# Where the mixing norm's scale per token is multiplied in, in a fp32 kernel of a three-block network

## The reference, cut to what matters

```python
def rmsnorm(x, w):
    xf = x.astype(jnp.float32)
    y = xf * lax.rsqrt(jnp.mean(xf * xf, axis=-1, keepdims=True) + EPS)
    return (y * w.astype(jnp.float32)).astype(x.dtype)

def second_block(x, norm_mix_w, w_in, ...):
    h = x                                   # x is layer_norm(DN_ALPHA * x + y, ln_g, ln_b)
        hn = rmsnorm(h, norm_mix_w[i])      # the mixing norm
        proj = hn @ w_in[i]
        q, k, v, z, xbc, dt_raw = jnp.split(proj, SPLITS, axis=-1)
        att = chunk_band_attention(q, k, v, rel_bias[i])
        ssd = ssd_mixer(z, xbc, dt_raw, conv_w[i], conv_b[i], dt_bias[i], ...)
        h = h + jnp.concatenate([att, ssd], axis=-1) @ w_out[i]
```

## Time and profile before

| what | value |
|---|---|
| time, 3 runs | 786.69, 787.38 (median), 789.47 us |
| the profiled execution's own time | 786.68 us |
| its span in the trace | 784.9 us (1.8 us lie around it) |
| PE, DVE, ACT, POOL busy | 98%, 66%, 53%, 12% of the span |
| PE's granted clock, mean | 0.997 of full speed |
| the seam, from the last product of the second layer to the first of the convolution's | 435.50 to 452.50 us |

### The profile page before, as it was taken

The page is one execution under the profiler, slowest core; times in us unless marked ns, Lnnn a source line. Parts: engine busy times, 40 slices in busy tenths (PEclk is TensorE's granted clock), DMA queues, the critical chain, the costliest instruction groups (busy, mean ns, idle before and its releaser), DMA issues.

```text
span 784.9 us, 13096 instructions
## 1 busy us (share of the span) xinstructions
PE 770.0 (98%) x5084; PEld 676.7 (86%) x5084; DVE 514.9 (66%) x816; ACT 414.7 (53%) x623; POOL 95.6 (12%) x69
## 2 busy tenths in 40 slices
PE   8999999999999999999999899999999999999997
PEld 8998877799988887999787799899777999999996
DVE  6995656666664658478866774886756755555554
ACT  5544445454664453445765667466655544444443
POOL 2241000000100013111400208500000000000002
PEclk9999999999999999999999999999999999999999
DMA  9865643344754644776732464643216576556541
GB/s 331 316 221 174 209 161 110 118 163 114 225 205 161 208 147 134 230 229 197 250 87 82 160 210 131 198 136 134 101 60 215 189 222 208 183 193 206 174 158 53
DMA packets 77051, 137.43 MB, mean 175 GB/s; under 512 B 7104, under 2 KB 15552, under 8 KB 76992
## 3 DMA queue, kind: packets, MB, share of 16 engines
q1 hardware_dynamic: 75744, 132.15, 51.9%
q0 software_dynamic: 1248, 4.46, 1.7%
HBM read 132.80 MB, written 1.05 MB: 171 GB/s over the span
## 4 chain that ended last, share of the span: by engine, by line
PE 89%; DVE 4%; issue 2%; POOL 2%; ACT 1%; DMA 1%; SPq 0%; POOLq 0%; ACTq 0%; DVEq 0%
PE acc L1069 13%; PE acc L1071 13%; PE acc L1070 13%; PE acc L1077 12%; PE acc L1079 12%; PE acc L1078 12%; PE acc L1357 1%; DVE w_lo L798 1%; PE acc L1391 1%; DMA raw<-in_w_in_even 1%; PE acc L1341 1%; PE acc L1330 1%; PE acc L1270 1%; PE acc L1226 1%; PE acc L1452 1%
## 5 line engine op out<-in xcount | busy, mean ns | idle before, releaser
L798 DVE TENSOR_TENSOR w_lo<-raw,w_hi 128x1024 fp32r<-128x1024 f32 (+1 forms) x224 | 276.1, 1250 | 165.9 <-ACT w_hi L778 86.2
L1077 PE MATMUL acc<-x_hi,w_hi 128*128 128x256 f32 x840 | 234.9, 280 | 1.2 <-DVE w_lo L798 0.8
L1079 PE MATMUL acc<-x_hi,w_lo 128*128 128x256 f32 x840 | 232.2, 276 | 0.0
L1078 PE MATMUL acc<-x_lo,w_hi 128*128 128x256 f32 x840 | 232.1, 276 | 0.0
L778 ACT ACTIVATE w_hi<-raw 128x1024 fp32r<-128x1024 f32 (+1 forms) x128 | 133.4, 1044 | 127.5 <-PE acc L1079 64.0
L768 ACT ACTIVATE w_hi<-raw 128x1024 fp32r<-128x1024 f32 x109 | 116.0, 1065 | 108.9 <-PE acc L1079 55.4
L1077 PEld LDWEIGHTS acc<-x_hi,w_hi 128*128 128x128 f32 x840 | 157.7, 188 | 4.7 <-issue 3.5
L1078 PEld LDWEIGHTS acc<-x_lo,w_hi 128*128 128x128 f32 x840 | 157.8, 188 | 0.8 <-issue 0.5
L1079 PEld LDWEIGHTS acc<-x_hi,w_lo 128*128 128x128 f32 x840 | 157.7, 188 | 0.0
L1069 PE MATMUL acc<-w_hi,cat_hi 128*128 128x512 f32 x272 | 109.0, 401 | 0.2 <-DVE w_lo L798 0.2
L1071 PE MATMUL acc<-w_hi,cat_lo 128*128 128x512 f32 x272 | 106.2, 391 | 0.0
(11 more groups left out here) (297 smaller groups left out, 911.9 us busy)
## 6 DMA issues: line engine op xcount, KB each, us to landing
raw<-in_w_ff SPq DMA_DIRECT2D x32, 1024.0 KB, 5.3
raw<-in_w_in_even SPq DMA_DIRECT2D x28, 1024.0 KB, 5.0
raw<-in_w_in_odd SPq DMA_DIRECT2D x16, 1024.0 KB, 5.4
raw<-in_w_in SPq DMA_DIRECT2D x16, 1024.0 KB, 5.6
raw<-in_w_out_even SPq DMA_DIRECT2D x12, 1024.0 KB, 5.8
raw<-in_w_out SPq DMA_DIRECT2D x4, 1024.0 KB, 5.0
raw<-in_w_in_even SPq DMA_DIRECT2D x4, 512.0 KB, 6.6
raw<-in_w_ukv_even SPq DMA_DIRECT2D x8, 256.0 KB, 3.2
```

What stands on the lines that cost most here:

```text
L798: ins = eng.tensor_tensor(lo, r, hi.bitcast(F32), ALU.subtract)
L1077: pe.matmul(o, wh[k][:, fs], hi[:, ka, :], start=start and f % 2 == 0, stop=False, skip_group_check=True)
L1078: pe.matmul(o, wh[k][:, fs], lo[:, ka, :], start=False, stop=False, skip_group_check=True)
L1079: ins = pe.matmul(o, wl[k][:, fs], hi[:, ka, :], start=False, stop=stop, skip_group_check=True)
```

## The change

The rows are no longer multiplied by r ahead of the transposes. PE transposes `res` itself as soon as `row_normed` has written it (semaphore `mix_row`), the high and low parts and all products of the last block's input are those of the unscaled norm, and r comes in where a product is read:

- v (both halves): ACT's copy, one instruction per 128 tokens with r as its scale. z: ACT's tanh takes r/2 as its scale, and y*z in `finish` takes r as a third factor.
- The convolution's input, q and k have features on partitions and tokens along the row, so r must lie along the row: DVE writes a diagonal of r (`mix_diag`), PE multiplies ones with it (`mix_spread`), ACT copies the result to `r_row`. DVE reads these chunks and multiplies by `r_row`, where ACT read them before.
- dt: DVE's sum with the bias is split per 128 tokens, with r as a scalar.

The order moves as well. The two squares, r and the mean squares now stand behind the transposes' high parts or the low parts. v's products are in `v_rows`: for the first tokens the high*high and high*low ones, then the second tokens' turn, then the rest. dt's products are one part of 256 tokens behind v. `keep_busy` runs no matmuls ahead of the first turn (5 before) and 4 ahead of the second (1 before). The four transposes of a half share a bank, and each 128 tokens have banks of their own.

```diff
-BUSY_MIX = (5, 1)
+BUSY_MIX = 4
...
     step("mix_turn", 1)
-    step("rows_of", (rows_pieces["dt"], 0, 0, 8))
     step("rows_of", (rows_pieces["v"], 1, 0, 8))
...
         else:
+            step("mix_spread", 0)
             step("dt_sum", c_dt)
...
+    for c in chunks:
+        c.scaled = c.acts == "x" and c.n >= after_mix and c.epilogue != "relu2"
...
+            def v_rows(p, t):
+                def high(u, b):
+                    pe.wait_ge(*due("mix_hi", 4 * u + b + 1))
+                    for k in (2 * b, 2 * b + 1):
...
+                        pe.matmul(o, xh, wh[k], start=k == 0, stop=False)
+                        pe.matmul(o, xh, wl[k], start=False, stop=False)
+                def low(u, b):
+                    pe.wait_ge(*due("mix_lo", 4 * u + b + 1))
...
+                if t == 0:
+                    for b in range(4):
+                        high(0, b)
+                    return
+                for b in range(4):
+                    low(0, b)
+                    high(1, b)
+                for b in range(4):
+                    ins = low(1, b)
...
             def mix_turn(t):
                 if t:
-                    pe.wait_ge(*due("mix_lo", 4))
-                    keep_busy(acc[:, v_piece.chunk.pair, 1, :], BUSY_MIX[1])
-                rows = tmp[:, t * D:(t + 1) * D]
+                    keep_busy(acc[:, v_piece.chunk.pair, 1, :], BUSY_MIX)
                 for h in range(2):
-                    pe.wait_ge(*due("mix_scaled", 2 * t + h + 1))
+                    pe.wait_ge(*due("mix_row", 2 * t + h + 1))
...
-                elif kind == "mix_rows":
-                    keep_busy(aux[:, 3, :], BUSY_MIX[0])
+                elif kind == "mix_spread":
+                    pe.wait_ge(*due("mix_diag", 1))
+                    own(pe.matmul(aux[:, 3, 0:S], ones, gated[:, 1, :], start=True, stop=True), "mix_spread")
...
-            def row_scaled(t):
...
                 elif kind == "mix_turn":
                     row_hi(i)
                     if i == 0:
+                        row_squares(0, 1)
+                        hi_prep(act, own, dt_piece.n)
                         hi_first(act, own, conv_piece.n)
-                        row_squares(1)
-                        row_scaled(1)
                     else:
+                        row_squares(1, 0)
+                        row_squares(1, 1)
                         hi_rest(act, own, conv_piece.n)
...
+                    if c.scaled and c.epilogue == "copy_tok":
                         act.wait_ge(*due("piece_used", c.pieces[-1].n + 1))
+                        act.wait_ge(*due("mix_r", T))
+                        for t in range(T):
+                            ins = act.activation(epi_dst(c)[:, t], a2[:, t], ACT.Copy, scale=mix_r[:, t:t + 1])
+                        own(ins, "acc_read_act")
...
+                    elif c.epilogue == "conv_in":
+                        dve.wait_ge(*due("piece_used", c.pieces[-1].n + 1))
+                        dve.wait_ge(*due("row_scale", 1))
+                        for b in range(2):
+                            ins = dve.tensor_tensor(conv_in[:, f:f + 2, 3:], a2[:, b, :].rearrange("p (f s) -> p f s", f=2), rows_scale(2), ALU.mult)
...
+                    elif c.scaled and c.epilogue == "copy_feat":
+                        own(dve.scalar_tensor_tensor(dst.rearrange("p (f s) -> p f s", f=4), a2.rearrange("p b (f s) -> p (b f) s", f=2), scale, rows_scale(4),
+                                                     ALU.mult, ALU.mult), "acc_read_dve")
...
                     row_centred(1)
-                    row_lo(0, 0, 2)
                     row_normed(1)
-                    row_lo(0, 2, 4)
+                    row_lo(0)
+                    row_mean_square(0)
+                    row_lo(1)
+                    low_prep(dt_piece.n)
                     row_mean_square(1)
-                    low_prep(dt_piece.n)
-                    row_lo(1, 0, 4)
                     low_prep(conv_piece.n)
...
+                elif kind == "mix_spread":
+                    dve.wait_ge(*due("mix_r", T))
+                    for t in range(T):
+                        ins = dve.tensor_scalar(gated[:, 1, t * P:(t + 1) * P], ident, mix_r[:, t:t + 1], None, ALU.mult)
+                    own(ins, "mix_diag")
+                    own(dve.tensor_scalar(half_r, mix_r, 0.5, None, ALU.mult), "mix_half")
```

More of the change, by code:

```diff
@@ L542, in build @@
             c = s[1]
-            c.reader = "act" if c.info.get("table") == 1 else READER.get(c.epilogue, "dve")
+            c.reader = "act" if c.info.get("table") == 1 else "dve" if c.scaled and c.layout == "feat" else READER.get(c.epilogue, "dve")
             reads[c.reader] += 1
@@ L1129, in rows_of @@
                 hi, lo = acts[c.acts]
-                if p is c.pieces[0] and t == 0:
+                if p is c.pieces[0] and (t == 0 or p is dt_piece):
                     before = by_turn[c.turn - 2]
@@ L1136, in rows_of @@
                 pe.wait_ge(*due("lo_ready", n_dve[p.n]))
-                ts = slice(t * P, (t + 1) * P)
+                ts = slice(0, S) if p is dt_piece else slice(t * P, (t + 1) * P)
+                if p is v_piece:
+                    v_rows(p, t)
+                    return
                 if p.order == "beside":
@@ L1484, in _, with row_squares @@
             scratch = probs.rearrange("p a n -> p (a n)")[:, 0:D]
-            def row_squares(t):
-                for h in range(2):
-                    act.wait_ge(*due("mix_row", 2 * t + h + 1))
-                    if t and h == 0:
-                        act.wait_ge(*due("mix_squared", 2))
-                    hs = slice(h * NCOL, (h + 1) * NCOL)
-                    own(act.activation(scratch[:, hs], res[:, t, hs], ACT.Square, scale=D ** -0.5, accum_out=stats[:, 38 + 2 * t + h:39 + 2 * t + h]),
-                        "mix_squared")
+            def row_squares(t, h):
+                act.wait_ge(*due("mix_row", 2 * t + h + 1))
+                if t and h == 0:
+                    act.wait_ge(*due("mix_squared", 2))
+                hs = slice(h * NCOL, (h + 1) * NCOL)
+                own(act.activation(scratch[:, hs], res[:, t, hs], ACT.Square, scale=D ** -0.5, accum_out=stats[:, 38 + 2 * t + h:39 + 2 * t + h]),
+                    "mix_squared")
             def last_squares(t, c0, c1, at):
@@ L1585, in _ @@
                     a2 = acc[:, c.pair, :, 0:c.width] if c.layout == "tok" else acc[:, c.pair, :, :]
-                    if c.epilogue in ("copy_tok", "copy_feat"):
+                    if c.scaled and c.epilogue == "copy_tok":
                         act.wait_ge(*due("piece_used", c.pieces[-1].n + 1))
-                        scale = DH ** -0.5 if c.acts == "x" and c.info["dst"] == ("R3", 0) else 1.0
-                        own(act.activation(epi_dst(c), a2, ACT.Copy, scale=scale), "acc_read_act")
+                        act.wait_ge(*due("mix_r", T))
+                        for t in range(T):
+                            ins = act.activation(epi_dst(c)[:, t], a2[:, t], ACT.Copy, scale=mix_r[:, t:t + 1])
+                        own(ins, "acc_read_act")
+                    elif c.scaled and c.epilogue == "silu_tok":
+                        act.wait_ge(*due("piece_used", c.pieces[-1].n + 1))
+                        act.wait_ge(*due("mix_half", 1))
+                        for t in range(T):
+                            ins = act.activation(epi_dst(c)[:, t], a2[:, t], ACT.Tanh, scale=half_r[:, t:t + 1])
+                        own(ins, "tanh_ready")
+                    elif c.epilogue in ("copy_tok", "copy_feat") and not c.scaled:
+                        act.wait_ge(*due("piece_used", c.pieces[-1].n + 1))
+                        own(act.activation(epi_dst(c), a2, ACT.Copy), "acc_read_act")
                     elif c.epilogue.startswith("silu"):
@@ L1612, in _ @@
                     elif c.epilogue == "conv_in":
-                        act.wait_ge(*due("piece_used", c.pieces[-1].n + 1))
                         act.wait_ge(*due("pad_ready", 1))
-                        for b in range(2):
-                            f = c.info["dst"] + 2 * b
-                            ins = act.activation(conv_in[:, f:f + 2, 3:], a2[:, b, :].rearrange("p (f s) -> p f s", f=2), ACT.Copy)
-                        own(ins, "acc_read_act")
-                        own.wait()
+                        act.wait_ge(*due("acc_read_dve", c.read_count))
                         m = c.info["dst"] // 4
@@ L2008, in _ @@
                         dve.wait_ge(*due("dt_summed", 1))
-                        v = ssd_c[:, 0, :].rearrange("p (t n) -> p t n", t=T)
-                        own(dve.tensor_tensor(v, a2[:, 1, 0:32].rearrange("p (t n) -> p t n", t=T), cst[:, C_DT:C_DT + 16].rearrange("p (a n) -> p a n", a=1).to_broadcast([P, T, 16]),
-                                          ALU.add), "acc_read_dve")
+                        for t in range(T):
```

(5 more changed lines are left out.)

71 lines of the change are left out of this document (43 added, 28 removed).

## The result

| | kernel before | changed kernel |
|---|---|---|
| median (lowest to highest), 10 runs each | 786.71 us (785.96 to 789.47) | 792.51 us (789.37 to 795.04) |
| ratio, 95% interval | | 1.0074 [1.0063, 1.0085] |
| profiled execution: time, span | 786.68, 784.9 us | 792.25, 790.4 us |
| mean granted clock of PE | 0.997 | 0.994 |
| PE, DVE, ACT, POOL busy | 98, 66, 53, 12% | 98, 66, 52, 12% |

The forecast was +2.75 us, the median moved by +5.8. The busy shares don't show it, the waits of PE do. First the seam on PE (columns as in the earlier trace rows), up to the end of the first convolution piece.

A forecast was written before the change was run, and what follows sets the result against it. PE, busy 98% of the span, was taken to bound the kernel. The terms -3.7 + 2.9 + 0.45 + 1.5 + 0.5 + 1.1 = +2.75 us on 786.68 gave 789.4 us, with an 8-in-10 range of 784.8 to 792.5.

The forecast's parts named there:

- term 1: Seam from second layer to convolution: without the wait for r and ACT's scaling, first convolution product comes 3.7 us earlier.
- term 6: Scan: q and k reads move to DVE; k's second chunk delays the band's first scores, +1.1 us.
- Term 2: End of first convolution piece: PE waits for DVE's diagonal, queued behind a low part, +2.9 us.
- Term 3: End of first convolution piece: the added matmul of ones times the diagonal, +0.45 us.
- Term 4: Convolution behind the wait for the diagonal: PE's clock falls to 1.2 GHz, +1.5 us.
- Term 5: Convolution's reads move to DVE: the third delays the last silu and PE's later transposes, +0.5 us.
- Rival B: Seam: the clock falls there as well, slowing v's products, +2.85 us on the sum, 792.3 us; chance 0.20.
- Rival D: Seam: v's copy waits longer for the second r and holds the convolution, 790.4 us at one us; chance 0.05.
- Rival A: Diagonal ready when PE arrives, so the seam's gain is kept, -1.65 us, 785.0 us; chance 0.10.
- Rival C: Wait for the diagonal exists, but the clock stays up and DVE has slack, neutral, 786.3 us; chance 0.20.

The follow-up runs named there:

- e4: Changed kernel with the second tokens' mean square moved ahead of the last two of DVE's sixteen low parts; 792.89 us, ratio 1.0077.
- e5: Changed kernel with the edits of e1, e3 and e4 together; 783.9 us, ratio 0.9968.
- e8: e5 with DVE's centring of a row split into two halves of 512; 783.95 us, ratio 0.9965.
- e1: Changed kernel with DVE writing the diagonal and half of r ahead of the second convolution piece's low parts; 786.52 us, ratio 1.0002.
- e2: Changed kernel with dummy products on PE in two waits, six before the diagonal, four before the band's first scores; 790.03 us, ratio 1.0045.
- e3: Changed kernel with DVE's scaled read of k's second chunk moved into its wait for POOL's inverse deviation; 790.69 us, ratio 1.0047.
- e6: e5 with DVE's six odd convolution taps ahead of the scaled read of the next chunk; 783.73 us, ratio 0.996.
- e7: Changed kernel without the four dummy products ahead of the seam's second set of transposes; 791.95 us, ratio 1.0063.

## Why the prediction was wrong

The forecast was 789.4 us; the result lies at 792.5. The mechanism and the sign of each of the six terms were right; one term was mis-sized, and a consequence of another was left out. By the segments the change costs +6.25 for +2.75: of these 3.5 us, 1.5 are term 1, 1.6 the fall of the clock behind term 6, and the rest is spread over small ones. The profile shows +5.5 because its seam happened to begin 0.76 earlier.

- **Term 1, -3.7; measured -2.19.** The step that failed is "POOL takes 0.54", and with it "the copy ends near 448.5": it ended at 449.50. The shape of everything else was right: e4 and e5, which take only that delay away, show -3.75. A row for a better price was in the trace. The earlier trace rows have POOL at 0.54 and at 1.52. What DVE did at 439.45, the start of the 1.52, stands in no row that I had written down:

```profile
439.29 1.27 DVE L1857 SCALAR_TENSOR_TENSOR tmp<-res,stats,R 128x1024 f32<-128x1024 f32 x1
```

It is the centring, with two SBUF inputs, and POOL ended 0.41 us behind it (440.97 against 440.56). I had moved the operation from DVE's idle time (444.23) to just ahead of 2.35 us of such work, and priced it as if it still lay in the idle time. An estimate from these rows, with my own times: the mean square at 446.8, two low parts to 449.2, r 0.4 later at 449.6, v's copy to 450.4; that is 1.6 later than 448.8, and the sum would have been about +4.35. The rule stands in the Trainium skill, "SBUF — State Buffer", "Who interferes with whom": a DVE instruction with two SBUF inputs contends with a GpSimd instruction that reads SBUF. The traces agree: 2.62 and 0.54 us for one operation (e4), 1.52 and 0.98 (e8).
- **Term 2, +2.9; measured 3.12** (9.11 - 5.99 with e1), of which the profile shows 2.80 as idle. **Term 3, +0.45; measured 0.44** (5.99 - 5.55).
- **Term 4, +1.5; measured 1.64,** and shown to be the wait's doing by e1 and e2. It varies: 3.0 in the profile of e3 and 3.15 in that of e4, and by their mean clock four of the changed kernel's ten executions had no such fall.
- **Term 5, +0.5; measured 0.44.** That DVE's added work causes it rests on the timelines; e6 shows that the place of the taps behind the read, which I blamed, is not the lever.
- **Term 6, +1.1; measured 1.13** (e3). What I left out, the second step that failed, is what this wait does next. I gave the wait of 2.9 us a term for the clock, and at the scores, where my own list forecast a wait of about 1.7, none. It cost 1.61 in the profile. The earlier trace rows already had the clock falling behind waits of 0.51 and 1.75.
- **Rival B (792.3) has the right number for the wrong reason.** The clock stayed at 1.00 through the seam. The rule cited for it, in the Trainium skill, "TensorE: Matmul & The Clock Gate", "A second HAM failure mode: psum-queue depth-cycling", that small waits between groups make the clock go back and forth, does not show here: v's high products, paced by ACT's high parts, ran at full clock with PE busy for 11.6 of the 14 us from 436 to 450, and in e7 even the products behind a wait of 2.42 us did. What transposes alone do to the clock stays untested, since products lie between the seam's two groups of them.
- **Rival D** is what term 1 ran into: r held v's copy and the copy held the convolution. I gave it 0.05 and named no row that would make r late: what was late was neither the squares nor the mean square, but POOL's operation on them.
- **Rival A,** no wait for the diagonal: forecast at 785.0, measured in e1 at 786.5, 1.5 above by the late r.
- **Rival C,** neutral: the clock stayed up in four of ten executions, as it wanted, but DVE had no slack (terms 5 and 6), and even these four took 789.4 us or more.

The changed kernel's executions fit the same account: four of ten have a mean clock of 0.998 or 0.999 and spans of 787.5 to 788.9; the other six 790.4 to 793.1 at 0.992 to 0.996. Without any loss of clock the segments give -2.19 + 3.56 + 0.44 + 0.06 + 1.13 = +3.0 against before, with both losses +6.25.

## What to carry to other kernels

Price a small operation of GpSimd by what VectorE does beside it, not by its own duration elsewhere; if its result is waited for, raise it ahead of VectorE's operations with two SBUF inputs. When an operation or its result moves from one engine to another, write down the queue of the new engine row by row: three rows of VectorE in the wrong place cost more than the whole idea brought, and the same idea with these rows moved is 3 us faster than before. Each new wait of TensorE of a microsecond or two gets two terms, the wait and a possible fall of the clock behind it, the second with a chance.

## What the runs showed of the hardware

- An identical wait brings TensorE's clock down in some executions and not in others. Behind 2.80 us the fall began 1.8 us after work resumed in the changed kernel and within the wait itself in e3 and e4, for 1.64, 2.98 and 3.15 us lost (what the segment to the dt sum has above 9.11 and the next above 38.69: 0 + 1.64, 0.43 + 2.55, 0.46 + 2.69). Behind 1.74 us it fell in the profiles of the changed kernel, e1, e4 and e7, but by their mean clock most executions of e1 have one fall fewer than that profile. Behind 2.42 us it did not fall (e7). In the kernel before it fell behind 0.51 and 1.75 us. The Trainium skill, "TensorE: Matmul & The Clock Gate", Part 1, says that the chip's observation runs freely and does not start with the kernel, so that the moment of a change depends on where the work happens to fall. The different moments behind the same 2.80 us fit this; no run tests it.
- Dummy products in a wait held the clock at 1.00 (e2), at no cost to the wait (9.09 for 9.11 us, 6.54 for 6.59): 2.5 us on the medians.
- A power of one element per partition on GpSimd: 0.54 us beside VectorE's reads of PSUM or its idle time, 1.52 beside 1.27 us with two SBUF inputs, 2.62 beside 2.35 us of them, 0.98 beside the same 1.27 us of work cut in halves of 0.7. In the kernel before it also took 0.54 (from 436.98) beside moments of a row, 0.69 us with one SBUF input (from 436.93). Between the two halves of e8 it got in; between the two low parts that make up the 2.35 us it did not, and why stays open.
